# A gated decoder trunk on one core: the gating input projection by Strassen's seven products, its weight sums made by transfers in two parts

## The chip, the core and the metric

The kernel runs on one core of a Trainium2 chip. The metric is the device time of one execution in microseconds (us), as the median of several runs. The engines are TensorE (PE, with its weight loads as PEld), VectorE (DVE), ScalarE (ACT), GpSimd (POOL) and SyncE (SP, which here only starts transfers). "Bank" is one of the eight 128 x 512 accumulation banks of the tile `ps`.

## The reference, cut to what matters

The trunk has two layers on 512 tokens of 1024 channels: a conformer convolution with its feed-forward, then a chunked gating unit with its feed-forward, each followed by a residual sum and a layer normalization. The part that the change touches:

```python
def chunked_spatial_gating(x, w_in, b_in, ln_g, ln_b, w_s, b_s, w_out, b_out):
    z = jax.nn.gelu(x @ w_in + b_in, approximate=False)
    u, v = jnp.split(z, 2, axis=-1)
    v = layer_norm(v, ln_g, ln_b)
    ...
    s = jnp.einsum("gts,bnsgc->bntgc", w_causal, v) + b_s.T[:, :, None]
    s = s.reshape(bsz, t, GMLP_HALF)
    return (u * s) @ w_out + b_out
```

`x @ w_in` is 512 x 1024 by 1024 x 2048. Its second half of columns gives `v` (here "the first projection", since the kernel computes it first), its first half gives `u`.

## The kernel before, in words

All products keep float32 accuracy by splitting: ACT writes a rounded high part (`his`), DVE subtracts it for the low part (`los`), and PE does three matmuls (high-high, high-low, low-high) for each 128 x 128 by 512 block.

**Weights** are a stream of units of 128 x 1024. SP loads unit u into slot u mod 4 of `raw` once the low part of unit u-4 is written; `his` and `los` put its parts into `wh` and `wl`, rings of four, or, around a normalization, into early places (`eh`, `el`). PE signals `w_used` after each unit, which frees the ring slot. All queues are written out by hand, one block for each engine, and run in order.

**Strassen before the change.** The down projections of both feed-forwards are already done with seven products in place of eight. They need sums of weight quarters, made in device memory (`summed`) by transfers: plain copies from SP (`copies`), then accumulating transfers from POOL (`summed_weights`), paced by `w_used` during the up projection.

**The gating stage.** After the second normalization (n = 1) PE transposes the four token tiles of `res` back to feature-major (`block_fm`, 8 transposes each); ACT writes their high parts (`block_hi`), DVE their low parts (`block_lo`). Then PE does the first projection: `down_by_block(U_GV, 4, 4, ...)` for 512 columns, one token tile after another, 24 matmuls each, with the last two `block_fm` in between; then `down_by_k(U_GV + 4, 4, 0, ...)` for the other 512 columns. That is 8 units and 192 matmuls. DVE adds the bias row into `vtm` (eight additions of 128 x 512), ACT applies Gelu, DVE takes the statistics, and normalizes `v` tile by tile into `vh`, `vl`. Meanwhile PE does the second projection (`up`, eight units of 24 matmuls, `U_GU`), whose last two are each followed by two groups of the spatial product (`spatial`), and the first of these waits for all of `vl`. In the middle of the first projection DVE also adds the output bias row to `res` (`residual(2)`).

The quarters are named A11, A12, A21, A22 for tokens by input channels (second index: channels), and the same indices for the weights.

## Time and profile before

| | us |
|---|---|
| median of 3 runs (lowest, highest) | 1015.83 (1014.35, 1017.22) |
| profiled execution, its own time | 1015.58 |
| its span (first to last instruction) | 1013.8 |
| PE busy | 1003.6 |
| DVE busy | 867.6 |
| ACT busy | 604.5 |
| POOL busy | 233.3 |

Busy times are sums over the whole span. A matmul of 128 x 512 is shown as 389 ns long, but the next one starts 227 ns after it, so the duration of a row is not its price on PE; the distance of two starts is. A measurement tells a difference of about 0.3% from none.

### The profile page before, as it was taken

To read this page: it belongs to the slowest core of one execution; us is meant where nothing else is said; L and a number is where in the kernel's file an instruction comes from. 1 tells how busy PE (TensorE), PEld (TensorE's weight loads), DVE (VectorE), ACT (ScalarE), POOL (GpSimd) and SP (SyncE) were. 2 spreads that over 40 slices of the span, in tenths; PEclk is the share of its full clock that TensorE was granted. 3 is DMA by queue.
4 is the path that set the end of the run, shared out by engine and by line. 5 is a ranking of instruction groups with operands and counts; after the bars stand their busy time and mean duration, and the time that the engine had idled before them with its cause. 6 is when DMAs were issued, how large, how long until landed. Compare 5 with 4: busy or idle time off the path is not lost.

```text
span 1013.8 us, 15746 instructions
## 1 busy us (share of the span) xinstructions
PE 1003.6 (99%) x5379; PEld 861.1 (85%) x5379; DVE 867.6 (86%) x1228; ACT 604.5 (60%) x903; POOL 233.3 (23%) x289
## 2 busy tenths in 40 slices
PE   9999999999999999999999999999999999999997
PEld 7777788988899988888888888898988999888885
DVE  6999977897988988898894878779888888879888
ACT  7889865564565556666454343457555555566653
POOL 2998730023232121000010210002423212100001
PEclk9999999999999999999999999999999999999999
DMA  9766269369889676376555333825989966627652
GB/s 342 218 161 166 58 147 349 119 196 238 236 211 228 220 169 173 102 271 208 195 179 194 118 111 107 307 79 186 262 237 229 220 209 173 163 98 260 205 197 112
DMA packets 65590, 194.02 MB, mean 191 GB/s; under 512 B 7552, under 2 KB 8576, under 8 KB 65024
## 3 DMA queue, kind: packets, MB, share of 16 engines
q1 hardware_dynamic: 44144, 137.76, 39.1%
q0 software_dynamic: 19376, 48.24, 23.7%
q10 hardware_dynamic: 2016, 7.34, 2.1%
q8 instruction: 28, 0.46, 0.2%
q14 instruction: 26, 0.21, 0.1%
HBM read 178.11 MB, written 54.53 MB: 229 GB/s over the span
## 4 chain that ended last, share of the span: by engine, by line
PE 78%; DVE 5%; DMA 3%; issue 2%; ACT 1%; SPq 0%; DVEq 0%; POOL 0%; POOLq 0%; ACTq 0%
PE ps L2017 10%; PE ps L2018 10%; PE ps L2019 10%; PE ps L2306 6%; PE ps L2307 6%; PE ps L2308 6%; PE ps L2259 5%; PE ps L2260 5%; PE ps L2261 5%; PE ps L2027 4%; PE ps L2028 4%; PE ps L2029 4%; DMA raw<-d_weights 3%; PE ps L2186 1%; DVE ps L1618 1%
## 5 line engine op out<-in xcount | busy, mean ns | idle before, releaser
L2017 PE MATMUL ps<-xh,wh 128*128 128x512 f32 x528 | 208.5, 395 | 0.3 <-DVE wl L1280 0.3
L2018 PE MATMUL ps<-xl,wh 128*128 128x512 f32 x528 | 205.7, 390 | 0.0
L2019 PE MATMUL ps<-xh,wl 128*128 128x512 f32 x528 | 205.6, 389 | 0.0
L767 ACT ACTIVATE wh<-raw 128x1024 fp32r<-128x1024 f32 x114 | 119.9, 1057 | 80.4 <-PE ps L2308 49.5
L1280 DVE TENSOR_TENSOR wl<-raw,wh 128x1024 fp32r<-128x1024 f32 x101 | 123.2, 1224 | 32.9 <-ACT wh L767 32.5
L702 POOL DMA_DIRECT2D summed<-d_weights x88 | 75.2, 1115 | 198.0 <-PE ps L2019 96.4
L2017 PEld LDWEIGHTS ps<-xh,wh 128*128 128x128 f32 x528 | 99.2, 188 | 22.0 <-issue 1.2
L2019 PEld LDWEIGHTS ps<-xh,wl 128*128 128x128 f32 x528 | 99.1, 188 | 21.0
L2018 PEld LDWEIGHTS ps<-xl,wh 128*128 128x128 f32 x528 | 99.2, 188 | 20.7 <-issue 1.2
L2306 PE MATMUL ps<-wh,parts 128*128 128x512 f32 x264 | 102.9, 390 | 0.0
L2308 PE MATMUL ps<-wh,parts 128*128 128x512 f32 x264 | 102.7, 389 | 0.0
L2307 PE MATMUL ps<-wl,parts 128*128 128x512 f32 x264 | 102.7, 389 | 0.0
L1607 DVE TENSOR_TENSOR wl<-raw,wh 128x1024 fp32r<-128x1024 f32 x62 | 75.6, 1220 | 22.5 <-ACT wh L1014 22.5
L599 POOL TENSOR_SCALAR veps<-sqs 128x1 f32<-128x1 f32 x15 | 4.8, 323 | 385.2 <-ACT squares_down L961 266.2
L1376 DVE SCALAR_TENSOR_TENSOR ps<-glu,par,ps 128x512 f32<-128x512 f32 x125 | 84.7, 752 | 0.6 <-PE ps L2103 0.4
L622 POOL TENSOR_TENSOR gsum<-gsum,prods 128x512 f32<-128x512 f32 x53 | 70.2, 1324 | 14.5 <-ACT prods L836 8.4
L1014 ACT ACTIVATE wh<-raw 128x1024 fp32r<-128x1024 f32 x62 | 65.6, 1058 | 8.2 <-DMA raw<-d_weights 8.2
L1618 DVE SCALAR_TENSOR_TENSOR ps<-vpad,par,ps 128x512 f32<-128x512 f32 x80 | 60.3, 753 | 8.0 <-ACT ps L1038 2.2
L1618 DVE SCALAR_TENSOR_TENSOR ps<-gpad,par,ps 128x512 f32<-128x512 f32 x80 | 60.2, 753 | 6.4 <-DVE ps L1618 2.1
L2306 PEld LDWEIGHTS ps<-wh,parts 128*128 128x128 f32 x264 | 49.5, 188 | 11.1 <-DVE wl L1280 0.8
L2308 PEld LDWEIGHTS ps<-wh,parts 128*128 128x128 f32 x264 | 49.5, 188 | 10.4
L2307 PEld LDWEIGHTS ps<-wl,parts 128*128 128x128 f32 x264 | 49.6, 188 | 10.2
(266 smaller groups left out, 2543.9 us busy)
## 6 DMA issues: line engine op xcount, KB each, us to landing
raw<-d_weights SPq DMA_DIRECT2D x156, 512.0 KB, 4.9
raw<-summed SPq DMA_DIRECT2D x56, 512.0 KB, 4.1
summed<-d_weights POOLq DMA_DIRECT2D x88, 256.0 KB, 9.5
summed<-d_weights SPq DMA_DIRECT2D x66, 256.0 KB, 5.2
...
```

The source lines that it names most:

```text
L702: eng.dma_start(out, of, accum_op=ALU.add).then_inc(w_sum[i % AHEAD], 16)
L767: eng.activation(split_at(u)[0], raw[:, u % RAW, :], ACT.Copy).then_inc(w_hi, 1)
L1280: eng.tensor_tensor(l, raw[:, u % RAW, :], h.bitcast(f32), ALU.subtract).then_inc(w_lo, 1)
L1376: eng.scalar_tensor_tensor(out=ps[:, bank, :], in0=glu[:, j % 2, k:k + SEQ], scalar=par[:, c:c + 1], in1=ps[:, bank, :], op0=ALU.mult, op1 ...
L1607: eng.tensor_tensor(wl[:, slot, :], raw[:, part, :], wh[:, slot, :].bitcast(f32), ALU.subtract).then_inc(w_lo, 1)
L1618: eng.scalar_tensor_tensor(out=accs[v], in0=buf[:, off:off + SEQ], scalar=par[:, bass.ds(cw, 1)], in1=accs[v], op0=ALU.mult, op1=ALU.add). ...
L2017: eng.matmul(ps[:, bank, cols], a, xh[:, k, cols], start=(k == 0), stop=False)
L2018: eng.matmul(ps[:, bank, cols], a, xl[:, k, cols], start=False, stop=False)
L2019: mm = eng.matmul(ps[:, bank, cols], b, xh[:, k, cols], start=False, stop=(k == KD - 1))
L2306: eng.matmul(ps[:, bank + t, :], s_h, w_h[:, cols], start=first, stop=False)
L2307: eng.matmul(ps[:, bank + t, :], s_h, w_l[:, cols], start=False, stop=False)
L2308: mm = eng.matmul(ps[:, bank + t, :], s_l, w_h[:, cols], start=False, stop=last)
```

## The change

The first projection is done with Strassen's seven products (in Winograd's form): quarters of 256 tokens by 512 channels and of 512 channels by 512 columns, seven products of 24 matmuls each. The products need four sums of token quarters (`gn5` = A21 - A22, `gs2` = `gn5` - A11, `gs4` = `gs2` + A12, `gv7` = `gs2` + A22) and sums of weight quarters. The stream has 14 units for the projection in place of 8. The weight sums are made by transfers: SP copies three quarters during the convolution (`gv_copies`), POOL adds into them after the first normalization, and goes on behind the feed-forward's own sums. The first unit of the second projection moves in between the products, to bridge the making of the token sums. The bias addition to `res` moves from DVE to four accumulating transfers of POOL.

```diff
+GQ = KD // 2
+U_GU0 = U_GV + GQ + 2
+U_G56 = U_GU0 + 1
+U_G37 = U_G56 + GQ
+U_GU = U_G37 + GQ - 1
...
+        def gv_copies(i):
+
+            w1, w2 = weights_d[raw_gv + i], weights_d[raw_gv + GQ + i]
+            eng.dma_start(gsum_d[2 + i, :, 0:HALF], w1[:, 0:HALF]).then_inc(gv_copied, 16)
+            eng.dma_start(gsum_d[2 + GQ + i, :, HALF:UNIT], w2[:, 0:HALF]).then_inc(gv_copied, 16)
+            eng.dma_start(gsum_d[2 + GQ + i, :, 0:HALF], w2[:, HALF:UNIT]).then_inc(gv_copied, 16)
...
+            if 0 <= u - U_CONV_OUT < GQ:
+                gv_copies(u - U_CONV_OUT)
```

POOL, around the feed-forward's own sums, and in the gating stage:

```diff
+        eng.wait_ge(gv_copied, 16 * 3 * GQ)
+        eng.dma_start(fifth[:, :, first], w2[:, :, first], accum_op=ALU.add).then_inc(gv_sum, 16)
+        eng.dma_start(third[:, :, second], w2[:, :, second], accum_op=ALU.add).then_inc(gv_sum, 16)
+        eng.wait_ge(gv_sum, 16 * 2)
+        eng.dma_start(fifth[:, :, second], fifth[:, :, first]).then_inc(gv_sum, 16)
         up_sums(0)
+        eng.wait_ge(gv_sum, 16 * 3)
+        eng.dma_start(fifth[:, :, second], w2[:, :, second], accum_op=ALU.add).then_inc(gv_sum, 16)
...
+        for t in range(NT):
+            eng.dma_start(res[:, t, :], brow[:, :], accum_op=ALU.add).then_inc(res3_add, 16)
+        eng.wait_ge(w_used, U_GV + GQ)
+        eng.wait_ge(x_kept, 2 * NT)
+        eng.wait_ge(*lo_of(U_G56 + 1))
+        for t in range(NT // 2):
+            cols = slice(t * P, (t + 1) * P)
+            eng.wait_ge(ga_sum, 2 * t + 2)
+            eng.wait_ge(a22_kept, t + 1)
+            eng.tensor_tensor(gs4[:, :, cols], gs2[:, :, cols], a12f[:, :, cols], ALU.add).then_inc(ga_more, 1)
+            eng.tensor_tensor(gv7[:, :, cols], gs2[:, :, cols], a22f[:, :, cols], ALU.add).then_inc(ga_more, 1)
```

ACT, after the last `block_hi`:

```diff
+        eng.activation(brow[:, :], brow[:, :], ACT.Copy, scale=1.0 / ALPHA).then_inc(br3_ok, 1)
+        token_hi(gn5h, gn5, 0, ga_sum, 1)
+        token_hi(gs2h, gs2, 0, ga_sum, 2)
+        his([U_G56])
+        token_hi(gn5h, gn5, 1, ga_sum, 3)
+        token_hi(gs2h, gs2, 1, ga_sum, 4)
+        his([U_G56 + 1])
+        gelu_v(0, 0, G_C11 - 1)
+        gelu_v(1, 0, G_C11)
+        row(glb[:, :], R_GLB, gm_in)
+        his([U_G56 + 2])
+        gelu_u(0)
+        his([U_G56 + 3])
```

DVE, after the token sums:

```diff
+        token_lo(gn5l, gn5, gn5h, 0, 1)
+        token_lo(gs2l, gs2, gs2h, 0, 2)
+        los([U_G56])
+        los([U_G56 + 1])
+        token_lo(gn5l, gn5, gn5h, 1, 3)
+        token_lo(gs2l, gs2, gs2h, 1, 4)
+        los([U_G56 + 2])
+        eng.wait_ge(w_used, U_GU0)
+        eng.wait_ge(rows_ok, 1)
+        for t in halves:
+            eng.tensor_tensor(vtm[:, 2 + t, c2], vtm[:, 2 + t, c1], both_rows[:, :], ALU.subtract).then_inc(n_ok, 1)
+        eng.wait_ge(n_ok, NT // 2)
+        for t in halves:
+            eng.tensor_tensor(vtm[:, 2 + t, c1], ps[:, 4 + t, :], vtm[:, 2 + t, c1], ALU.add).then_inc(gv_rd, 1)
+        los([U_G56 + 3])
```

PE, after the products A11 x B11 and A12 x B21 (24 matmuls and a `block_fm` for each of two token tiles) and the product with A22 (24 matmuls):

```diff
+        up(split_at(U_GU0), GU_BANK[0]).then_inc(w_used, 1)
+        for pair in range(GQ // 2):
+            for t in range(NT // 2):
+                eng.wait_ge(ga_lo, 2 * t + 2)
+                for i in (2 * pair, 2 * pair + 1):
+                    u = U_G56 + i
+                    if t == 0:
+                        eng.wait_ge(*lo_of(u))
+                    gv(u, 0, 0, gn5p, i, t)
+                    mm = gv(u, 1, 2, gs2p, i, t)
+                    if t == 1:
+                        mm.then_inc(w_used, 1)
...
+        for i in range(GQ):
+            gv_third(i)
+            if i < GQ - 2:
+                gv_seventh(i)
```

Three places show what the change does to the order on the engines. On DVE in the gating stage, from the last normalized tile on, it stood like this before (`vtm` holds the projection, `wl<-raw,wh` is a `los`):

```order
L1772 SCALAR_TENSOR_TENSOR res<-scaled_down,rstd,brow_n 128x1024 [waits rstd_ok,nrm]
L1532 TENSOR_TENSOR xl<-ps,xh 128x4x128 [waits x_hi] x4
L1943 TENSOR_TENSOR vtm<-ps,gvrow 128x512 [waits blk,gv_in]
L1280 TENSOR_TENSOR wl<-raw,wh 128x1024 [waits w_hi,w_used]
L1943 TENSOR_TENSOR vtm<-ps,gvrow 128x512 [waits blk]
L1280 TENSOR_TENSOR wl<-raw,wh 128x1024 [waits w_hi,w_used]
L1948 BN_STATS stats<-vtm 128x6 [waits v_gelu]
```

After the change the same place reads as follows, from the second token tile's part of the sums on (`gn_133` is `gn5`, `gs_134` is `gs2`):

```order
L2091 TENSOR_TENSOR gs_134<-gn_133,a11f 128x4x128 [waits ga_sum]
L2070 TENSOR_TENSOR gn5l<-gn_133,gn5h 128x4x128 [waits ga_hi,ga_sum]
L2070 TENSOR_TENSOR gs2l<-gs_134,gs2h 128x4x128 [waits ga_hi]
L1407 TENSOR_TENSOR wl<-raw,wh 128x1024 [waits w_hi,w_used] x2
L2070 TENSOR_TENSOR gn5l<-gn_133,gn5h 128x4x128 [waits ga_hi]
L2070 TENSOR_TENSOR gs2l<-gs_134,gs2h 128x4x128 [waits ga_hi]
L1407 TENSOR_TENSOR wl<-raw,wh 128x1024 [waits w_hi,w_used]
L2103 TENSOR_TENSOR vtm<-vtm,both_rows 128x512 [waits rows_ok,w_used]
L2103 TENSOR_TENSOR vtm<-vtm,both_rows 128x512
L2106 TENSOR_TENSOR vtm<-ps,vtm 128x512 [waits n_ok]
L2106 TENSOR_TENSOR vtm<-ps,vtm 128x512
L1407 TENSOR_TENSOR wl<-raw,wh 128x1024 [waits w_hi,w_used]
```

The low part of the fourth of these units (the last row, `U_G56 + 3`) now stands behind six operations on the tokens and on `vtm`. On POOL, between the roots of the second normalization and the mask of the spatial weights, there was nothing; now there stand four transfers and four additions (`gs_135` is `gs4`, `gv_136` is `gv7`):

```order
L639 TENSOR_TENSOR rstd<-veps,half_m 128x1 [waits eps_ok]
L814 DMA res<-brow 128x1024 [waits xt,x_ok,br3_ok]
L814 DMA res<-brow 128x1024 x3
L822 TENSOR_TENSOR gs_135<-gs_134,a12f 128x4x128 [waits ga_sum,w_lo,a22_kept,x_kept,w_used]
L823 TENSOR_TENSOR gv_136<-gs_134,a22f 128x4x128
L822 TENSOR_TENSOR gs_135<-gs_134,a12f 128x4x128 [waits a22_kept,ga_sum]
L823 TENSOR_TENSOR gv_136<-gs_134,a22f 128x4x128
L826 AFFINE_SELECT wsraw<-wsraw 128x1024 [waits gm_in]
```

What moved here is work that DVE did before (the addition of the row) or that is new; DVE's queue holds the rest. On ACT, from the last high parts of the tokens on, it now reads:

```order
L1063 ACTIVATE a22f<-ps 128x4x128 [waits x_lo]
L855 DMA bsrow<-d_rows 128x1024 [waits x_ok]
L855 DMA grow<-d_rows 128x1024
L855 DMA brow_n<-d_rows 128x1024
L1343 ACTIVATE brow<-brow 128x1024 [waits bo_in]
L1327 ACTIVATE gn5h<-gn_133 128x4x128 [waits ga_sum]
L1327 ACTIVATE gs2h<-gs_134 128x4x128 [waits ga_sum]
L850 ACTIVATE wh<-raw 128x1024 [waits raw_in2,w_used]
L1327 ACTIVATE gn5h<-gn_133 128x4x128 [waits ga_sum]
L1327 ACTIVATE gs2h<-gs_134 128x4x128 [waits ga_sum]
L850 ACTIVATE wh<-raw 128x1024 [waits raw_in3,w_used]
L1332 ACT_TABLE_LOAD
```

Before, this stretch of ACT held six row transfers and the table load, then Gelu and `his` in turn; the high parts of the token sums and three more weight units now go through it.

## Rows read from the trace of the kernel before

**Rows 1.** The page: the span, and PE's busy time.

```profile
span 1013.8 us, 15746 instructions
PE 1003.6 (99%) x5379; PEld 861.1 (85%) x5379; DVE 867.6 (86%) x1228; ACT 604.5 (60%) x903; POOL 233.3 (23%) x289
```

**Rows 2.** PE's waits between 480 and 640 us: total, times, longest.

```profile
PE ps L2351 <- DVE wl L1280: 0.2, 1, 0.2
```

**Rows 3.** Timeline of PE in the gating stage: start, us, engine, line, what.

```profile
537.90 0.47 PE L2027 MATMUL ps<-eh,xh 128*128 128x512 f32 x1
...
538.68 0.39 PE L2027 MATMUL ps<-eh,xh 128*128 128x512 f32 x1
...
560.44 0.39 PE L2027 MATMUL ps<-wh,xh 128*128 128x512 f32 x1
```

**Rows 4.** Timeline of DVE in the gating stage, with idle time before.

```profile
533.79 1.29 DVE L1772 SCALAR_TENSOR_TENSOR res<-scaled_down,rstd,brow_n 128x1024 f32<-128x1024 f32 x1 [0.89 <-POOL rstd L588]
...
538.38 1.29 DVE L1532 TENSOR_TENSOR xl<-ps,xh 128x512 fp32r<-128x512 f32 x2 [2.11 <-ACT xh L967]
...
565.64 2.35 DVE L1280 TENSOR_TENSOR wl<-raw,wh 128x1024 fp32r<-128x1024 f32 x2
```

**Rows 5.** Timeline of ACT in the gating stage (ACTq: transfers it starts).

```profile
539.52 0.45 ACTq L772 DMA_DIRECT2D bsrow<-d_rows  x1
...
541.40 1.28 ACT L1232 ACT_TABLE_LOAD   x1 [2.56 <-issue]
...
555.58 2.00 ACT L767 ACTIVATE wh<-raw 128x1024 fp32r<-128x1024 f32 x2
...
571.57 1.23 ACT L1232 ACTIVATE vtm<-vtm 128x512 f32<-128x512 f32 x2 [5.10 <-DVE vtm L1943]
```

**Rows 6.** DVE and POOL side by side: durations in ns, min/median/max, first and last start.

```profile
L743 POOL TENSOR_SCALAR_AFFINE_SELECT wsraw<-wsraw x1: 1680/1680/1680, 559.6 to 559.6; 128x1024 f32<-128x1024 f32 x1
L1548 DVE SCALAR_TENSOR_TENSOR res<-res,brow x4: 1214/1214/2124, 560.2 to 564.5; 128x1024 f32<-128x1024 f32 x4
L588 POOL TENSOR_TENSOR rstd<-veps,half_m x2: 538/540/543, 528.4 to 533.1; 128x1 f32<-128x1 f32 x2
L588 POOL TENSOR_TENSOR rstd<-veps,half_m x4: 1407/1462/1558, 578.2 to 584.6; 128x1 f32<-128x1 f32 x4
```

**Rows 7.** POOL's additions of 128x512 in the convolution, columns as above.

```profile
L622 POOL TENSOR_TENSOR gsum<-gsum,prods x53: 1270/1296/2317, 21.0 to 111.8; 128x512 f32<-128x512 f32 x53
```

**Rows 8.** Timeline of DVE: v's normalization from first to last, and the first use of the spatial product.

```profile
577.90 1.27 DVE L1962 SCALAR_TENSOR_TENSOR vtm<-vtm,mv,glg 128x1024 f32<-128x1024 f32 x1
...
597.86 1.23 DVE L1970 TENSOR_TENSOR vl<-vtm,vh 128x1024 fp32r<-128x1024 f32 x1
...
609.79 0.69 DVE L1982 TENSOR_TENSOR vtm<-ps,bsrow 128x512 f32<-128x512 f32 x1 [3.34 <-PE ps L2401]
```

**Rows 9.** Convolution: timelines of POOL, SP and PE.

```profile
90.06 0.87 POOL L613 DMA_DIRECT2D wl<-raw  x1
96.91 0.80 SPq L532 DMA_DIRECT2D raw<-d_weights  x2
99.04 0.48 PE L2017 MATMUL ps<-xh,wh 128*128 128x512 f32 x1
```

**Rows 10.** Stretch: length, busy of PE, PEld, DVE, ACT, POOL; clock, DMA share, GB/s.

```profile
150.00:180.00 30.00, 29.70 (x143) 24.36 (x142) 24.28 (x38) 17.94 (x29) 2.23 (x6) 1.00 0.99 335
```

**Rows 11.** Timeline of POOL: its first weight sums, and its return after the last.

```profile
217.86 5.95 POOL L702 DMA_DIRECT2D summed<-d_weights  x7 [32.77 <-issue]
510.45 0.19 POOL L599 TENSOR_SCALAR veps<-sqs 128x1 f32<-128x1 f32 x1 [120.22 <-ACT squares_down L961]
```

**Rows 12.** Stretches at the end of the program, columns as in Rows 10.

```profile
1006.00:1008.00 2.00, 1.00 (x5) 0.49 (x3) 1.97 (x4) 0.08 (x1) 0.00 (x0) 1.00 0.65 260
1008.00:1010.00 2.00, 0.00 (x0) 0.00 (x0) 1.72 (x5) 0.73 (x2) 0.88 (x2) 0.87 0.66 268
```

**Rows 13.** Weight loads from start to landing at 516 to 625 us.

```profile
DMA to landing us min/median/max: 3.0/3.3/6.0
```

310 lines of the change are left out of this document (235 added, 75 removed).

## The prediction, made before the changed kernel ran

> **What bounds the kernel now.** I read the page first: PE is busy for 1003.6 of a span of 1013.8 us [rows 1], DVE for 867.6. Then PE's waits in the stretch of the change, 480 to 640 us: one, of 0.2 us [rows 2]. So here the time is PE's instruction stream and nothing else, and DVE and ACT only have to be early enough. The price of a matmul is the distance of starts: 96 of them between 538.68 and 560.44 us, 0.2267 us each [rows 3]. All sums are made in the profiled execution (span 1013.8, its own time 1015.58) and carried to the median 1015.83, which is 0.25 us above it. About 0.3%, 3.05 us, is what a measurement tells from no change.
>
> **What PE saves.** The first projection falls from 192 to 168 matmuls; transposes, second projection and spatial products stay. 24 x 0.2267 = 5.44 us. This is the most that the change can give, and it is given only if PE never waits for the new work.
>
> **What is added.** Six more weight units: six loads, six `his` on ACT (two in 2.00 us [rows 5], 1.0 each) and six `los` on DVE (two in 2.35 us [rows 4], 1.15 apart). On DVE: twenty reads of banks and rows into `vtm` in place of eight, four token differences, eight low parts of token sums, all of 128x512 (two in 1.29 us [rows 4], 0.6 apart), less the four `residual` additions of 1.2 us: 6 x 1.15 + 24 x 0.6 - 4.9 = 16.4 us more. On ACT: 6 x 1.0 and about 15 short ones at 0.6. Both engines have room in total; what counts is the order.
>
> **PE's needs after the change.** Up to 537.90 us, where the last transposes end [rows 3], PE's stream is the same length. Then, with 24 matmuls as 5.44 us: the product with A22 from 537.9 to 543.4, the moved unit to 548.9, the first half of products five and six to 554.4, six matmuls of the second half to 555.8, and there it needs the low part of unit `U_G56 + 3`.
>
> **DVE and ACT up to there.** The last `normed` starts at 533.79 because it waits 0.89 us for its root [rows 4]; the first `vtm` addition fits into that gap. Then one addition (0.6), `block_lo` of tile 2 (1.2) and two `los` bring DVE to 539.1 and the last `block_lo` to 540.3. The unit for A22 is there at 538.0 and the last tile 0.5 us before PE asks for it: I take 0.2 us of wait here. Two additions and a `los` end at 542.7, four token differences at 545.4.
> ACT copies A22's second tile until 541.1, starts three row transfers (539.52 to 541.40 before, 1.9 us [rows 5]) until 543.0, scales `brow` until 544.0, and then does two token parts and a unit (546.2), two and a unit (548.4), the table load of 1.28 us, two Gelus of together 1.23, a transfer's start (0.4, nearest row 0.45) [rows 5] and the third unit: 552.4. DVE follows: the second unit's low part at 549.6, when PE wants it at 550.3. So far no wait.
> Without anything in its way DVE would then do two token parts (550.8), the third unit (552.5 to 553.6), two subtractions with `both_rows` (554.8), two bank additions (556.1) and the fourth unit: 557.3. PE would wait 1.5 us, from 555.8.
>
> **But POOL is in its way.** POOL's additions `gs4` and `gv7` wait for that same second low part, so all four start at 549.6 (the four transfers ahead, 0.9 us each by the nearest POOL issue [rows 9], are done by 548). The nearest row of such an addition is 1.296 us [rows 7]. What happens beside DVE: the mask on POOL ran from 559.55 to 561.23, and the DVE addition with both inputs in SBUF that started at 560.2 took 2.124 us against 1.214 for the other three, ending about as late as if it had begun when POOL was done. The other way too: POOL's roots take 0.54 us, and 1.41 to 1.56 while DVE runs such instructions [rows 6]. So the two take turns. The Trainium skill, SBUF — State Buffer, section "Who interferes with whom", has the rule: a DVE instruction with two SBUF inputs and a GpSimd instruction that reads SBUF exclude each other, and the second to issue blocks fully. The trace agrees, with its 0.91 us.
> Token parts, `los` and the `both_rows` subtractions all have two SBUF inputs. In turns, 1.15 us for each POOL addition and 0.55 or 1.1 for each DVE one: first token part 550.1, POOL 551.3, second token part 551.9 (PE wanted it at 551.7: 0.2 us), POOL 553.0, third unit 554.1 (in time for 554.6), POOL 555.3, subtraction 555.9, POOL 557.0, subtraction 557.6, bank additions (no SBUF pair, free) 558.8, fourth unit 560.1. PE comes to it at 556.0 and waits 4.1 us.
>
> **After it.** PE goes on at 560.1, does 18 matmuls to 564.2. POOL's last sum at 557.0 gives ACT's part at 558 and two units by 560.1; DVE has four token parts and two `los` done at 564.8, the first of these at 563.7, in time. The seventh product ends at 575.1; DVE reads its banks until 577.5, and two more units, a pair of statistics ahead, are in time by over 1.5 us. Loads land in 3.3 us, at most 6.0 [rows 13]; with the 2 MB of residual transfers beside them they may take longer, and the first that could hurt is needed 6 us after it is issued. From 577.5 DVE has a unit, six statistics, a unit and the aggregates (1.15 + 3.6 + 1.15 + 0.4) before v's normalization, which starts at 583.8; its 21.2 us, 577.90 to 599.1 before [rows 8], then end at 605.0. PE starts the spatial product after six units, 575.1 + 32.6 = 607.7, which leaves 2.7 us. (Before, DVE saw it at 609.79 [rows 8].)
>
> **The transfers.** The twelve copies start with units 16 to 19 in the convolution. The low part of units 14 and 15 is itself a transfer of POOL, issued at 90.06, and is down at 96.91, when SP goes on; PE uses it from 99.04 [rows 9]: 2.1 us to spare. Six copies, 1.57 MB, fall just ahead of it; at 335 GB/s, the rate of the busiest stretch with such copies [rows 10], they take 4.7 us, of which some 3.4 fit into idle transfer time: 1.3 us late, still in time. I cost it at nothing, with 2 us at the worst. The second piece has POOL's 32.77 idle us up to 217.86 for about 3 MB, the third its 120 idle us up to 510.45 [rows 11]. Both are hidden; POOL would have to be 15 us slower to be late with the feed-forward's own sums.
>
> **The sum.** -5.44 + 0.2 + 0.2 + 4.1 = -0.9 us: 1014.9 us. Both ends for the unknown price of the turns: nothing (the wait is 1.5), or all four additions in full with DVE idle meanwhile (5.2 more, the wait 6.7). Net -3.7 to +1.5.
>
> **The rivals.**
> *DVE is not held up* (chance 0.30): the additions on POOL start later than I think, or are short beside DVE, as the median of 1.296 us with a busy DVE in the convolution could hint; there DVE's instructions read a bank, though. Then -5.44 + 0.2 + 1.5 = -3.7: 1012.1 us, and 1011 if ACT is half a microsecond earlier at each row transfer.
> *The clock falls during the wait* (0.18), which decides for slower. At the end of the program PE stops at 1007.0 and the mean clock between 1008 and 1010 is 0.87 [rows 12], so it fell to its half, 1.2 GHz, at 1009.5, after 2.5 us without a matmul. A wait of 4.1 us in the middle may do the same, and each matmul at the lower level costs 0.227 us more. Twelve of them give 1017.6, a whole unit of 24 gives 1020.3; from 18 on (4.0 us over -0.9) the kernel is slower than before by more than 3.05 us. Against it: the wait is short, and PE was at its full rate up to it.
> *The copies in the convolution hold up unit 14* (0.10): 2 us or more on top, 1017 us.
>
> **The numbers.** Forecast as reckoned 0.42, own range 1013.3 to 1016.5. Faster by over 0.3%: most of the first rival and the lower edge of the forecast, 0.32. Slower: half of the clock's case, half of the copies', a little of the forecast, 0.16. Within 0.3%: 0.52. Range 1011.3 to 1018.0.
>
> **What would show it.** 24 fewer matmuls, surely. PE: one idle time of 3 to 5 us before a matmul that waits for the low part of unit `U_G56 + 3`, some 18 us after the last transposes; under 1.5 us there and the first rival holds. POOL's four additions and DVE's token parts and `los` between 549 and 558 us: durations stretched to about twice show the turns, plain 0.7 and 1.2 refute them. Clock under 1.00 behind the wait: the second rival. PE idle at about 99 us for `wl<-raw`: the third. I am wrong altogether if PE waits longest elsewhere: at the A22 product, or at the spatial product for v.

## The result, and the profile after

| | before | after |
|---|---|---|
| median of six executions each, us | 1015.49 | 1020.77 |
| lowest, highest | 1014.35, 1017.22 | 1017.82, 1023.90 |
| profiled execution, its own time | 1015.58 | 1017.82 |
| its span | 1013.8 | 1016.0 |

The ratio is 1.0052, with a 95% interval of 1.0032 to 1.0072. The change costs about 5.3 us (3.2 to 7.3), where I forecast a gain of 0.9. The profiled execution of the kernel after is the fastest of its six, 3 us under their median, and the one before lies at its median; what is read from the two traces is therefore compared piece by piece below, and not by their total times. The page of the kernel after, beside [rows 1]:

```profile
span 1016.0 us, 15812 instructions
PE 999.7 (98%) x5355; PEld 858.0 (84%) x5355; DVE 887.9 (87%) x1254; ACT 618.9 (61%) x924; POOL 256.6 (25%) x310
```

PE has its 24 matmuls less and is busy for 3.9 us less, and the span is longer all the same. So time went into waits, or lies where PE no longer works. PE's waits between 500 and 640 us (total, times, longest), beside [rows 2]:

```profile
PE ps L2579 <- DVE wl L1407: 3.1, 1, 3.1
PE ps L2537 <- DVE wl L1407: 1.0, 2, 0.7
PE ps L2579 <- DVE el L1407: 0.9, 1, 0.9
```

The first is the wait that the prediction named: low part of unit `U_G56 + 3`. PE's timeline around it:

```profile
555.79 0.39 PE L2581 MATMUL ps<-wh,gs2l 128*128 128x512 f32 x1
559.32 0.65 PE L2579 MATMUL ps<-wh,gn5h 128*128 128x512 f32 x1 [3.15 <-DVE wl L1407]
559.77 0.63 PE L2580 MATMUL ps<-wl,gn5h 128*128 128x512 f32 x1
...
562.75 0.48 PE L2581 MATMUL ps<-wh,gn5l 128*128 128x512 f32 x1
563.07 0.39 PE L2579 MATMUL ps<-wh,gs2h 128*128 128x512 f32 x1
```

Two things are to be seen. The next matmul starts 3.53 us after the last one, 3.30 more than the usual 0.23. And then the starts stand 0.43 us apart, not 0.23, up to 563.07: nine steps took 3.75 us where nine times 0.2267 are 2.04, so 1.71 us are lost behind the wait. The stretches of the same place (length, busy of PE, PEld, DVE, ACT, POOL; clock, DMA share, GB/s) show the reason in the clock:

```profile
555.00:560.00 5.00, 1.85 (x8) 1.21 (x7) 4.97 (x7) 2.84 (x5) 1.26 (x1) 0.95 1.06 277
560.00:565.00 5.00, 5.00 (x17) 3.94 (x17) 4.04 (x5) 1.06 (x1) 0.00 (x0) 0.71 1.04 282
```

A distance of 0.43 us is that of the lower of the clock's two levels, 1.2 GHz, and 0.23 that of the higher, 2.4 GHz.

What made PE wait is on DVE, whose timeline stands beside POOL's here:

```profile
548.79 0.68 DVE L2070 TENSOR_TENSOR gn5l<-gn,gn5h 128x512 fp32r<-128x512 f32 x1
549.39 1.78 DVE L2070 TENSOR_TENSOR gs2l<-gs,gs2h 128x512 fp32r<-128x512 f32 x1
551.10 2.31 DVE L1407 TENSOR_TENSOR wl<-raw,wh 128x1024 fp32r<-128x1024 f32 x1
553.33 3.48 DVE L2103 TENSOR_TENSOR vtm<-vtm,both_rows 128x512 f32<-128x512 f32 x2
556.85 1.29 DVE L2106 TENSOR_TENSOR vtm<-ps,vtm 128x512 f32<-128x512 f32 x2
558.05 1.22 DVE L1407 TENSOR_TENSOR wl<-raw,wh 128x1024 fp32r<-128x1024 f32 x1
...
549.10 1.52 POOL L822 TENSOR_TENSOR gs<-gs,a12f 128x512 f32<-128x512 f32 x1 [2.48 <-issue]
550.59 1.73 POOL L823 TENSOR_TENSOR gv<-gs,a22f 128x512 f32<-128x512 f32 x1
552.28 2.27 POOL L822 TENSOR_TENSOR gs<-gs,a12f 128x512 f32<-128x512 f32 x1
554.52 1.74 POOL L823 TENSOR_TENSOR gv<-gs,a22f 128x512 f32<-128x512 f32 x1
```

The merged row of the two subtractions, taken apart (durations in ns, min/median/max):

```profile
L2103 DVE TENSOR_TENSOR vtm<-vtm,both_rows x2: 1780/1780/1781, 553.3 to 555.0; 128x512 f32<-128x512 f32 x2
```

While POOL's four additions run, DVE's instructions take 1.78 in place of 0.68, 2.31 in place of 1.22, and each of the two subtractions 1.78 in place of 0.68: 1.1 us for each of the four additions. And each ends 0.55 us (128 x 512) or 1.1 us (128 x 1024) after the addition beside it has ended, about what it takes alone. That is taking turns, as forecast. The bank additions start at 556.85, when POOL's last addition has ended (556.26), so their plain length says nothing about turns. The rule of the Trainium skill on which the forecast leaned (SBUF — State Buffer, section "Who interferes with whom") holds here for POOL's tensor_tensor against DVE instructions with two SBUF inputs.

The loss that was not forecast at all begins 50 us earlier, with the second normalization. The same rows of DVE's timeline, of the kernel before, and then of the kernel after with POOL's row beside them:

```profile
505.45 0.69 DVE L1782 SCALAR_TENSOR_TENSOR res<-ps,res 128x512 f32<-128x512 f32 x1 [0.33 <-PE ps L2308]
...
509.11 0.42 DVE L1800 TENSOR_TENSOR parts<-made,parts 128x256 fp32r<-128x256 f32 x1
509.45 0.68 DVE L1782 SCALAR_TENSOR_TENSOR res<-ps,res 128x512 f32<-128x512 f32 x1
```

```profile
503.61 0.69 DVE L1909 SCALAR_TENSOR_TENSOR res<-ps,res 128x512 f32<-128x512 f32 x1 [0.33 <-PE ps L2494]
...
507.28 1.52 DVE L1927 TENSOR_TENSOR parts<-made,parts 128x256 fp32r<-128x256 f32 x1
508.72 0.68 DVE L1909 SCALAR_TENSOR_TENSOR res<-ps,res 128x512 f32<-128x512 f32 x1
...
506.45 2.07 POOL L807 TENSOR_TENSOR both_rows<-gvrow 128x512 f32<-128x512 f32 x1 [91.81 <-PE ps L2494]
```

The kernel after comes to this place 1.84 us early and leaves it 0.73 early. In between, an operation of 0.42 us took 1.52, beside POOL's sum of the two halves of the bias row: turns again. The rest follows on PE (before, then after):

```profile
518.60 0.60 PE L2186 MATMUL ps<-ident,res 128*128 128x128 f32 x4
...
530.70 0.55 PE L2186 MATMUL ps<-ident,res 128*128 128x128 f32 x3
```

```profile
517.88 1.03 PE L2372 MATMUL ps<-ident,res 128*128 128x128 f32 x8
...
527.58 0.50 PE L2579 MATMUL ps<-eh,xh 128*128 128x512 f32 x1 [0.93 <-DVE el L1407]
...
531.11 1.03 PE L2372 MATMUL ps<-ident,res 128*128 128x128 f32 x8
...
538.24 0.48 PE L2579 MATMUL ps<-wh,xh 128*128 128x512 f32 x1
...
1006.57 0.39 PE L2539 MATMUL ps<-xh,parts 128*128 128x512 f32 x1
```

0.72 us early at the first transposes, 0.41 late at the third; between them is a wait of 0.93 us for `el`, the low part of `U_GV + 3`. The last matmul starts at 1006.57, and before at 1006.61: inside the program the whole gain of 5.44 us has been given back. And behind it there is one loss more. The rows of the program's last line, before and after (engine, duration in ns three times, start):

```profile
L2426 POOLq DRAIN  x1: 3749/3749/3749, 1009.3 to 1009.3; - x1
...
L2426 SPq DRAIN  x1: 7/7/7, 1013.6 to 1013.6; - x1
L2426 SPq EVENT_SEMAPHORE  x1: 17/17/17, 1013.8 to 1013.8; - x1
```

```profile
L2680 POOLq DRAIN  x1: 6650/6650/6650, 1009.2 to 1009.2; - x1
...
L2680 SPq DRAIN  x1: 7/7/7, 1013.5 to 1013.5; - x1
L2680 SPq EVENT_SEMAPHORE  x1: 17/17/17, 1016.0 to 1016.0; - x1
```

POOL's last instruction starts at the same time and takes 6.65 us in place of 3.75. In the kernel before it ended at 1013.03, ahead of SP's last instruction at 1013.6; now all engines wait for it at the program's end, and the span ends 9.5 us after the last matmul's start in place of 7.2 (2.24 us more).

The ledger of the two profiled executions, from 505 us on: +1.11 (bias row on POOL), +1.14 (`el`), -0.07 up to 538.24, -5.44 (24 matmuls), +3.30 (wait), +1.71 (clock), +2.24 (POOL's last instruction) is +3.99. The kernel after had come to 505 us 1.84 us early, which leaves 2.15; the spans differ by 2.2. That head start is chance: the second trace of the same kernel (a1 below) was 3.6 us late from 268 us on. But behind 500 us it says the same as the first: from there to the last matmul it loses 1.82 us against the kernel before, the first trace 1.80, and each loses 2.24 or 2.25 more at the end.

### The profile page after: what moved, and what is told of

Read it like the earlier page. It is cut to its first block, busy times and chain, and to the rows that moved or that the text cites. A ratio compares the mean times of both kernels' runs of the same rounds, so it can differ in the third digit from the quotient of the medians.

```text
span 1016.0 us, 15812 instructions
## 1 busy us (share of the span) xinstructions
PE 999.7 (98%) x5355; PEld 858.0 (84%) x5355; DVE 887.9 (87%) x1254; ACT 618.9 (61%) x924; POOL 256.6 (25%) x310
## 4 chain that ended last, share of the span: by engine, by line
PE 80%; DVE 6%; issue 2%; DMA 1%; ACT 1%; POOL 0%; DVEq 0%; POOLq 0%; ACTq 0%
PE ps L2204 11%; PE ps L2205 11%; PE ps L2206 11%; PE ps L2446 6%; PE ps L2447 6%; PE ps L2445 6%; PE ps L2492 6%; PE ps L2493 6%; PE ps L2494 6%; PE ps L2214 2%; PE ps L2215 2%; PE ps L2216 2%; DVE wl L1407 1%; PE ps L2579 1%; PE ps L2372 1%
## 5 line engine op out<-in xcount | busy, mean ns | idle before, releaser
L850 ACT ACTIVATE wh<-raw 128x1024 fp32r<-128x1024 f32 x120 | 126.0, 1057 | 82.5 <-PE ps L2494 49.5
L1407 DVE TENSOR_TENSOR wl<-raw,wh 128x1024 fp32r<-128x1024 f32 x107 | 131.0, 1231 | 21.9 <-ACT wh L850 21.9
L1729 DVE TENSOR_TENSOR wl<-raw,wh 128x1024 fp32r<-128x1024 f32 x62 | 75.6, 1220 | 19.8 <-ACT wh L1104 19.8
L1104 ACT ACTIVATE wh<-raw 128x1024 fp32r<-128x1024 f32 x62 | 65.5, 1057 | 7.0 <-DMA raw<-d_weights 7.0
```

Source lines behind the costliest of these rows:

```text
L850: eng.activation(split_at(u)[0], raw[:, u % RAW, :], ACT.Copy).then_inc(w_hi, 1)
L1407: eng.tensor_tensor(l, raw[:, u % RAW, :], h.bitcast(f32), ALU.subtract).then_inc(w_lo, 1)
L1729: eng.tensor_tensor(wl[:, slot, :], raw[:, part, :], wh[:, slot, :].bitcast(f32), ALU.subtract).then_inc(w_lo, 1)
```

## The experiments

The kernel before ran beside each of them, and ratios are to its runs there; its medians lay between 1015.21 and 1015.94 us (1014.41 beside f3, a single execution). The theory: DVE and POOL take turns, that gives the long wait, the clock's fall hangs on the wait, and something of its own lengthens the program's end. The rival: the transfers of the sums cost the time, by contention in the convolution, at the loads, and at the end.

**a1_again.** The changed kernel once more, unchanged.

> The changed kernel once more, with nothing altered, for a second trace of it. By every theory about 1020.8 us, 5 us over before. Turn theory (DVE and POOL exclude each other, PE waits for the low part of unit U_G56 + 3, then its clock falls): the same wait of 3 us before that unit's first matmul and a clock below 1.00 behind it, together some 5 us. Load theory (the four residual transfers hold up weight loads): the high parts of the three units after it come 2 to 5 us late, and how late differs from execution to execution, which would explain that most executions took 3 us more than the profiled one.

Measured: 1021.25 us, ratio 1.0050 (1.0036 to 1.0064). The wait was 3.16 us, and seven matmuls behind it stood 0.43 us apart. The loss is real, and the wait is the same in both traces.

**a2_lo_first.** The low part of `U_G56 + 3` ahead of the bias subtractions and bank additions on DVE:

```diff
         los([U_G56 + 2])
+        los([U_G56 + 3])
...
-        los([U_G56 + 3])
```

> One line of DVE's queue moved: the low part of unit U_G56 + 3 stands right behind that of U_G56 + 2, ahead of the two subtractions with both_rows and the two bank additions. Turn theory: the low part is written about 3 us earlier, the wait shrinks from 3.1 us to under 1 us, and the clock stays at 1.00; 4 to 5 us faster than the changed kernel, about 1016. Load theory: its high part waits for its load until 553.5 us anyway, so PE gains only 1.5 to 2 us at that unit and then meets the next late units: 1018 to 1020.

Measured: 1020.88 us, ratio 1.0037 (1.0023 to 1.0051). The one wait became four of 0.77, 1.79, 0.79 and 0.67 us, 4.0 in all, and no matmul was slow. The order on DVE alone moves the wait; what DVE has to do up to the third product is too long. The clock is gained, but its gain went into the new waits: from 500 us to the last matmul this trace loses 1.99 us, no less than the changed kernel's 1.80.

**a3_late_res.** The residual's four transfers behind the roots of v's normalization:

```diff
-        for t in range(NT):
-            eng.dma_start(res[:, t, :], brow[:, :], accum_op=ALU.add).then_inc(res3_add, 16)
         eng.wait_ge(w_used, U_GV + GQ)
...
             mixer_root(ROOTS + 2 * NT + t, ROOTS + t + 1, t, 1)
+        for t in range(NT):
+            eng.dma_start(res[:, t, :], brow[:, :], accum_op=ALU.add).then_inc(res3_add, 16)
```

> The four residual transfers of POOL stand behind the roots of v's normalization, some 45 us later; nothing else. Turn theory: DVE's queue is as long as before and the wait before unit U_G56 + 3 stays near 3 us, the time stays within 1.5 us of the changed kernel's 1020.8. Load theory: loads land in 3 to 5 us again in place of 10 to 13, no high part waits for a load between 550 and 565 us, and the typical time falls by the 3 us by which most executions exceeded the profiled one, to about 1017.5.

Measured: 1021.76 us, ratio 1.0058 (1.0044 to 1.0071), with the wait still 3.14 us. The loads of weights between 538 and 560 us, from start to landing (least, median, most), first in the changed kernel and then in this one:

```profile
DMA to landing us min/median/max: 3.2/10.6/13.1
```

```profile
DMA to landing us min/median/max: 3.3/5.1/8.9
```

The transfers slow the loads to twice their time, but these are not what PE waits for. This one also shows that the wait alone doesn't decide the clock:

```profile
560.61 0.50 PE L2579 MATMUL ps<-wh,gn5h 128*128 128x512 f32 x1 [3.14 <-DVE wl L1407]
560.94 0.40 PE L2580 MATMUL ps<-wl,gn5h 128*128 128x512 f32 x1
```

With the same waits as the changed kernel and without the fall, this trace loses 0.19 us from 500 us to the last matmul, where the changed kernel loses 1.80. That puts the price of the fall at 1.6 us. In the other executions of this kernel it seems to have fallen: their mean granted clock is 0.994 in three and 0.996 in one, against 0.997 in the profiled one, and they took 3 to 6 us longer. No trace of them shows where.

**a4_fill.** Thirty small matmuls of no use, so that PE isn't idle in the wait:

```diff
                     if t == 0:
+                        if i == GQ - 1:
+                            busy(30, 7)
                         eng.wait_ge(*lo_of(u))
```

> PE does 30 transposes of the identity into a free bank (some 3 us of otherwise idle time) just before it waits for the low part of unit U_G56 + 3; they change no result. If the fall of the clock costs what the trace shows (nine matmuls at 0.43 in place of 0.23 us), this kernel is 1.7 to 2 us faster than the changed one although PE does more work, with the clock at 1.00 throughout; if the clock is no cause, it is equal or slower by up to 0.5 us.

Measured: 1019.97 us, ratio 1.0030 (1.0018 to 1.0041). The wait left was 0.6 us, and the clock stood at 1.00 in every stretch from 540 to 570 us. About 1.3 us against a1 come back in the medians, though the intervals overlap. In the trace the nine steps behind the wait are 1.5 us shorter, but 1.2 us of it went again at 576 and 578 us, where PE waited for low parts whose loads had come late (ACT waited 2.7 and 0.7 us for them). So the fall costs what it costs only where the next units are ready.

This execution was also the slowest of its ten, 1023.88 us, for a reason that has nothing to do with the edit. In the convolution, just where the prediction's third rival expected it, PE waited for the low part of unit 14, and the clock fell behind that wait too. The row of the wait, and the stretch behind it (columns as above):

```profile
102.55 0.50 PE L2204 MATMUL ps<-xh,wh 128*128 128x512 f32 x1 [2.12 <-DMA wl<-raw]
...
103.00:107.00 4.00, 4.00 (x12) 3.08 (x11) 4.00 (x7) 3.44 (x9) 1.92 (x2) 0.57 0.89 207
```

**b1_sums_only.** The rival alone: the kernel before with the sums' transfers and nothing that uses them.

```diff
             load(u % RAW, u)
+            if 0 <= u - U_CONV_OUT < GQ:
+                gv_copies(u - U_CONV_OUT)
...
+        eng.dma_start(fifth[:, :, first], w2[:, :, first], accum_op=ALU.add).then_inc(gv_sum, 16)
+        eng.dma_start(third[:, :, second], w2[:, :, second], accum_op=ALU.add).then_inc(gv_sum, 16)
...
         up_sums(0)
...
+        eng.dma_start(fifth[:, :, second], w2[:, :, second], accum_op=ALU.add).then_inc(gv_sum, 16)
...
```

> The kernel before, with the transfers of the weight sums added and nothing that uses them: SP's twelve copies in the convolution, GpSimd's three transfers at the first normalization and its ten behind the feed-forward's own sums. No computation differs from before. If the transfers cost nothing, as the prediction had it: 1015.5, ratio 1.000, and the program's last instruction comes about 7.2 us after the last matmul's start. If GpSimd's last instruction lengthens with the number of transfers that it issued (it took 3.75 us before, 6.65 us in each version of the changed kernel), this kernel ends some 2 us later, 1017.5, with matmuls that end as before. If the copies in the convolution hold up units 14 and 15 as well, some 1 to 2 us more at 105 us in some executions, 1018 to 1019.

Measured: 1018.33 us, ratio 1.0021 (1.0011 to 1.0031), 2.1 us. POOL's last instruction took 6.49 us, and the program ended 9.39 us behind the last matmul's start: 2.2 us more than before, which is the whole of the measured difference. (POOL's queue carries 167 transfers here, twelve more than before, where the expectations count thirteen.) In this trace the transfers cost nothing ahead of the last matmul, so the end part of the rival stands. Its contention part is not settled by this one trace. Between 90 and 115 us, where SP's copies run, the matmuls keep to the time of the kernel before within 0.02 us in all five other traces without the copies. In the fourteen traces with them they lose 0.7 us on average: nothing or 0.1 in six of them, 0.4 to 1.0 in six, 1.8 in a7 and 4.0 in a4, and every wait there is for `wl<-raw`. So the copies do cost something, in some executions and not in others.

**a5_no_sums.** The other way round: the changed kernel without them.

```diff
-                gv_copies(u - U_CONV_OUT)
...
-            return gsum_d[u - U_GV - GQ]
+            return weights_d[raw_gv + u - U_GV]
...
-            return gsum_d[u - U_G56 + 2]
+            return weights_d[raw_gv + (u - U_G56) % KD]
```

> The changed kernel without the transfers of the weight sums: units that read a sum load a plain block of the weights instead, so the gating's first projection multiplies by wrong weights, with the same number of loads, splits and matmuls. If the transfers carry part of the loss (GpSimd's last instruction 2.25 us, copies in the convolution about 1 us): 1017.5 to 1018.5. If they carry none, 1020.8. The wait for the low part of the fourth unit of the sums, 3.1 us, and the slower clock behind it stay in both cases.

Measured: 1019.11 us, ratio 1.0038 (1.0025 to 1.0052). All PE waits of the stage were as in the changed kernel (3.1, 0.9, 0.7), and POOL's last instruction took 6.49 us still. That was against my expectation for the end: without any transfer for the sums, the four residual transfers that remain are enough. The 2 us against a1 are within what the intervals leave open. As in a3 the clock stood at 1.00 behind a wait of 3.14 us, and from 500 us to the last matmul this trace loses 0.15 us.

**a6_rows_late.** POOL's sum of the bias row's halves behind the residual's transfers:

```diff
-        eng.wait_ge(gv_in, 16)
-        eng.wait_ge(w_used, U_GV - FOURTH)
-        eng.tensor_tensor(both_rows[:, :], gvrow[:, 0:HALF], gvrow[:, HALF:D], ALU.add).then_inc(rows_ok, 1)
         for t in range(NT):
             norm_root(ROOTS + NT + t, NT + t + 1, t)
...
+        eng.wait_ge(gv_in, 16)
+        eng.tensor_tensor(both_rows[:, :], gvrow[:, 0:HALF], gvrow[:, HALF:D], ALU.add).then_inc(rows_ok, 1)
```

> The changed kernel with GpSimd's sum of the two halves of the bias row moved from the start of the second normalization (506 us) to behind the residual's transfers (about 546 us). If that one instruction, 2.07 us beside VectorE's 128x256 operation that grew from 0.42 to 1.52 us, puts VectorE's whole normalization 1.1 us late: TensorE's shift between 500 and 531 us, +1.1 and +1.2 us, falls to under 0.5 in all and the time to 1018.8 to 1019.8, unless the sum now falls beside VectorE's work on the token sums and gives 1 us back there. If the shift comes from elsewhere (the bias row's load, the weights' loads): it stays, 1020.8.

Measured: 1021.56 us, ratio 1.0057 (1.0041 to 1.0073). The operation `parts<-made,parts` was back at 0.42 us, and TensorE's shift of 1.1 us between 505 and 518 us was gone; the wait for `el`, 0.9 us, stayed, so it has another cause. At its new place POOL's sum (second row) took turns again, and one DVE operation of 0.69 us (first row) took 2.57:

```profile
545.81 2.57 DVE L2090 TENSOR_TENSOR gs<-gn,a11f 128x512 f32<-128x512 f32 x1
...
546.55 2.96 POOL L813 TENSOR_TENSOR both_rows<-gvrow 128x512 f32<-128x512 f32 x1
```

PE's waits for `wl` rose to 5.0 us, 3.7 the longest. From 500 us to the last matmul this trace loses 3.49 us, 1.7 more than the changed kernel, although the 1.1 are gone: a cost that is moved into DVE's crowded stretch is paid there more than in full.

**a7_token_sums_dve.** The four token sums by DVE, and no longer by POOL:

```diff
+        for t in halves:
+            cols = slice(t * P, (t + 1) * P)
...
+            eng.tensor_tensor(gs4[:, :, cols], gs2[:, :, cols], a12f[:, :, cols], ALU.add).then_inc(ga_more, 1)
+            eng.tensor_tensor(gv7[:, :, cols], gs2[:, :, cols], a22f[:, :, cols], ALU.add).then_inc(ga_more, 1)
         eng.wait_ge(w_used, U_GU0)
```

> The changed kernel with the four token sums gs4 and gv7 formed by VectorE, ahead of its wait for the fourth product, instead of by GpSimd (1.5 to 2.3 us each there, between 549 and 556 us). If the two engines take turns in these operations, VectorE's own stretched ones (1.78 and 2.31 us, 0.69 and 1.22 alone, 3.48 for two subtractions) shrink by some 4 us while the four added ones cost about 2.8 us, and the wait of TensorE for the low part of the fourth unit falls from 3.1 to about 2: 1019 to 1020. If there are no turns and the long operations have another reason, VectorE's work is 2.8 us longer and so is the wait: about 6 us, 1024.

Measured: 1019.99 us, ratio 1.0043 (1.0028 to 1.0059). DVE's timeline, in place of the stretched one above:

```profile
552.93 0.68 DVE L2061 TENSOR_TENSOR gs2l<-gs,gs2h 128x512 fp32r<-128x512 f32 x1
...
554.60 1.23 DVE L1398 TENSOR_TENSOR wl<-raw,wh 128x1024 fp32r<-128x1024 f32 x1 [0.98 <-ACT wh L841]
555.75 0.68 DVE L2095 TENSOR_TENSOR gs<-gs,a12f 128x512 f32<-128x512 f32 x1
```

No operation is stretched: the turns are shown from both sides. The wait fell to 2.22 us, with no slow matmul behind it. Four additions of 0.60 us on DVE are cheaper than four of 1.5 to 2.3 in turns, but not by much, and now ACT waited 2.17 us, until 557.25, for the load of `U_G56 + 3`, so that the load was next.

**c1_one_transfer, c2_semaphores, f3_one_row, g1_one_fewer.** What lengthens POOL's last instruction? The kernel before with one transfer more on POOL's queue (c1: 256 KB, f3: one row), with twelve unused semaphores (c2), and with a transfer less (g1). The edit of c1:

```diff
         up_sums(0)
+        eng.dma_start(more_d[:, 0:HALF], weights_d[0, :, 0:HALF]).then_inc(more, 16)
```

> The kernel before with one more transfer on GpSimd's queue (a plain copy of 256 KB that nobody reads, behind the first feed-forward's sums): 156 transfers in place of 155. GpSimd's last instruction took 3.75 us in the kernel before (155 transfers on its queue), 6.49 in the changed kernel without the sums' transfers (159) and in the kernel before with them (168), 6.65 in the changed kernel (171). If it goes by the number of GpSimd's transfers, in steps: a step between 155 and 159 may lie here, 6.5, or just not, 3.75. If it goes by their bytes or packets: 3.75 to 4.0.

> The kernel before with twelve more semaphores that nothing uses. If GpSimd's last instruction goes by the number of semaphores of the program (two more in the kernel before with the sums' transfers, some fourteen in the changed kernel), it takes about 6.5 us here; if it goes by transfers, 3.75.

> The kernel before with one more transfer on GpSimd's queue, of one row of 2 KB: 156 transfers, but hardly more bytes or packets than before (19376 packets on that queue). If GpSimd's last instruction goes by the number of transfers, 6.5 us as in c1_one_transfer; if by packets or bytes (19456 packets in c1), 3.75.

> The kernel before with 154 transfers on GpSimd's queue: the residual of the last token tile ahead of the first normalization doesn't get its bias row, which is left out of the computation. If GpSimd's last instruction is short up to 155 transfers of this program: 3.75 us. If the kernel before with its 155 is a single case: 5.9 to 7.1 us.

One execution each. POOL's last instruction, in c1, f3, c2 and g1:

```profile
L2429 POOLq DRAIN  x1: 6483/6483/6483, 1007.8 to 1007.8; - x1
```

```profile
L2429 POOLq DRAIN  x1: 6487/6487/6487, 1008.7 to 1008.7; - x1
```

```profile
L2427 POOLq DRAIN  x1: 3749/3749/3749, 1008.1 to 1008.1; - x1
```

```profile
L2426 POOLq DRAIN  x1: 3749/3749/3749, 1009.4 to 1009.4; - x1
```

A single transfer more, even of one row, is the whole step of 2.7 us; twelve semaphores more do nothing. It isn't bytes.

**d1_mend.** Four edits against four losses: the bias row's sum by a transfer, TensorE taking both products of a unit at once, token sums on DVE, and the third unit of the sums for both token tiles ahead of the fourth.

```diff
-        eng.wait_ge(w_used, U_GV - FOURTH)
-        eng.tensor_tensor(both_rows[:, :], gvrow[:, 0:HALF], gvrow[:, HALF:D], ALU.add).then_inc(rows_ok, 1)
+        eng.dma_start(gvrow[:, HALF:D], gvrow[:, 0:HALF], accum_op=ALU.add).then_inc(rows_ok, 16)
...
                 mm = gv(U_GV + i, 0, 4, g11, i, t)
-            mm.then_inc(gv_pe, 1)
-            eng.wait_ge(c_rd, R_P4 + 1 + t)
-            for i in range(GQ):
+                if i == GQ - 1:
+                    mm.then_inc(gv_pe, 1)
                 mm = gv(U_GV + i, 1, 6, g12, i, t)
...
-        for pair in range(GQ // 2):
+        for units in ((0, 1), (2,), (3,)):
```

> The changed kernel with four edits, each against one loss: the sum of the bias row's halves by an accumulating transfer in place of GpSimd's instruction (1.1 us); TensorE takes each unit of the first product at once with its other half in the second product, so that U_GV+3 is needed as late as before (el wait, 0.9 to 1.2 us); the token sums by VectorE (0.5 us); the third unit of the sums for both token tiles ahead of the fourth (six matmuls more before the wait, 1.4 us, and with a shorter wait perhaps a clock that doesn't fall, 1.7 us). If these readings are right: 1021 - 1.1 - 1.1 - 0.5 - 1.4 - 0 to 1.7 = 1015.2 to 1016.9. If VectorE's work is the bound of the stage however it is ordered, the waits only move and it ends at 1018 to 1020. GpSimd's last instruction still takes 6.5 us or more in either case.

Measured: 1019.87 us, ratio 1.0047 (1.0033 to 1.0061), 3 us above what I expected. The shift of 1.1 us, the wait for `el` and the slow matmuls were gone, but there were four waits for `wl`: 1.64, 1.11, 0.57 and 0.86 us.

**d2_mend_more.** As d1, with the residual's transfers late as in a3, and with these two moves (ACT, then DVE; the second `los` goes in between the two halves of the token sums):

```diff
+        his([U_G56 + 2])
         gelu_v(0, 0, G_C11 - 1)
         gelu_v(1, 0, G_C11)
         row(glb[:, :], R_GLB, gm_in)
-        his([U_G56 + 2])
...
+        los([U_G56 + 3])
+        for t in (1,):
```

> The kernel of d1 with the residual's four transfers behind the roots of the gating's normalization, ScalarE's high part of the third unit ahead of its two Gelu, and VectorE's low part of the fourth unit ahead of half of the token sums and of the bank additions. If what is left of the wait for the fourth unit is its load, which landed at 557.2 beside the residual's transfers with ScalarE waiting 2.17 us for it, the wait falls under 0.5 us: 1 to 2 us better than d1, 1013.5 to 1015.5. If it is VectorE's total work, the same as d1, with waits at the next units instead.

Measured: 1016.53 us, ratio 1.0010 (1.0002 to 1.0019). PE didn't wait at the fourth unit at all; 1.64 us at 540 and 1.12 us at the third product were left. In a3 the late transfers gained nothing, and here the step from d1, of which they are one part of three, gained 3.3 us. Together with the 2.17 us for which ACT waited for a load in a7 this speaks for two causes one behind the other, turns first and loads next; which of the three parts gained how much was not separated.

**h4_fewer and e4_best.** Fewer transfers on POOL's queue, 144 in place of 171 (h4), and the same in d2 with 145 and one more move (e4): plain copies within the sums are replaced by base copies on SP's queue.

```diff
+            half = slice(HALF, UNIT) if i % 2 else slice(0, HALF)
+            eng.dma_start(to[2 * KQ + i // 2, :, half], w1[:, HALF:UNIT]).then_inc(w_copied[i], 16)
...
-                    issue(i, fourth_sum(to, i), to[i, :, second])
...
-                    issue(i, fourth_sum(to, i), w1[i, :, second], ALU.add)
+                    issue(i, fourth_sum(to, i), to[i, :, second], ALU.add)
```

> The changed kernel with 144 transfers on GpSimd's queue in place of 171: plain copies of sums are replaced by base copies of a block of the weights on SyncE's queue, onto which GpSimd's transfer adds the rest (7 transfers for the gating's sums in place of 12, 22 fewer for the feed-forwards' sums). If GpSimd's last instruction goes by the number: 3.75 us, the last instruction of the program 7.2 us behind the last matmul's start, 1020.8 - 2.25 = 1018.5. If only the sums' total matters: 6.5 us still, 1020.8.

> The kernel of d2_mend_more with 145 transfers on GpSimd's queue (in the manner of h4_fewer, one more for the bias row), and on VectorE the low parts that the third product needs ahead of the bias subtractions and bank additions, with TensorE's wait for these behind the first unit of the third product. From d2's 1016.5: last instruction -2.25, wait at the third product (1.12 us) -1.0: 1013.2, ratio 0.998, faster than the kernel before, if the causes found are the whole loss and the last instruction goes by the number of transfers. If it doesn't: 1015.5. If VectorE bounds the stage and the wait only moves on: 1 us more in each case.

Measured: 1030.98 us, ratio 1.0146 (1.0130 to 1.0161), and 1027.31 us, ratio 1.0111 (1.0096 to 1.0125). Both expectations failed, for the end and for the total. POOL's last instruction took 5.92 and 7.14 us, so it doesn't simply go by the number of transfers either. And the base copies, which I had taken for free, cost about 10 us between 243 and 277 us: loads of weights between 225 and 285 us took 3.4/10.6/21.5 us to land (least, median, most) in h4 against 3.8/6.6/12.8 in the kernel before, and PE stood for 5.45 us in one piece. The clock fell in that wait, with a mean of 0.51 between 268 and 275 us in h4, which makes up to 3 of the 10. More copies on the queue that also brings the weights were the worst edit of all.

**e5_best.** As d2, with DVE's low parts for the third product ahead of the bias work, and PE's wait for a free bank one unit later:

```diff
+        for t in halves:
+            token_lo(gs4l, gs4, gs4h, t, 4 + 2 * t + 1)
+            token_lo(gv7l, gv7, gv7h, t, 4 + 2 * t + 2)
+        los([U_G37])
...
-        eng.wait_ge(gv_rd, G_MP4)
         for i in range(GQ):
             gv_third(i)
+            if i == 0:
+                eng.wait_ge(gv_rd, G_MP4)
```

> The kernel of d2_mend_more with VectorE's low parts for the third product, and of its first unit, ahead of the bias subtractions and bank additions, and TensorE's wait for these behind the first unit of the third product. GpSimd's transfers as in d2 (172), so its last instruction stays at 6.7 us. From d2's 1016.5: the wait of 1.12 us at the third product gone, 1015.4, the same as the kernel before. If VectorE bounds the stage and the wait moves on to the next units: 1016.5.

Measured: 1015.99 us, ratio 1.0008 (0.9999 to 1.0017). The wait of 1.12 us was down to 0.28. The longest was now 1.64 us at 542, and it is one of my own edits: with both products of a unit taken together, the first one ends later for the second token tile, DVE's bank addition waits 1.91 us for it, and the low parts queued behind it are late.

**e6_best.** Both products of a unit together for the first token tile alone:

```diff
-                mm = gv(U_GV + i, 1, 6, g12, i, t)
-                if t == 1:
-                    mm.then_inc(w_used, 1)
+                if t == 0:
+                    if i == 0:
+                        eng.wait_ge(c_rd, R_P4 + 1)
+                    gv(U_GV + i, 1, 6, g12, i, t)
+            if t == 1:
+                eng.wait_ge(c_rd, R_P4 + 2)
+                for i in range(GQ):
+                    gv(U_GV + i, 1, 6, g12, i, t).then_inc(w_used, 1)
```

> The kernel of e5_best with TensorE taking the two products of a unit together for the first token tile alone; for the second tile the first product comes whole, as in the changed kernel, so that VectorE's bank addition isn't held back (1.91 us in e5) and U_GV+4's low part, 1.64 us late there, is in time. From e5's 1016.0: -1.6, 1014.4, ratio 0.999 and with it about 1 us faster than the kernel before, although GpSimd's last instruction still takes 6.7 us. If VectorE is the bound of the stage, the wait comes back at the fourth unit or the third product: 1016.

Measured: 1014.06 us, ratio to the kernel before 0.9986 (0.9976 to 0.9995), in the same comparison with 1015.87. PE's waits between 500 and 640 us:

```profile
PE ps L2581 <- DVE wl L1396: 0.2, 1, 0.2
PE ps L2539 <- DVE wl L1396: 0.2, 1, 0.2
```

So the losses found in the stage are nearly all of them: with each undone, the change is 1.8 us faster than before by the medians (1.4 by the ratio), even with POOL's last instruction still at 6.69 us.

The traces say it piece by piece. The table compares the start of the same matmul, counted from the first, with the kernel before: what is lost (+) from 90 to 115 us, from 500 us to the last matmul, and from there to the end of the span.

| run | 90 to 115 us | 500 us to last matmul | behind it |
|---|---|---|---|
| changed kernel | 0.0 | +1.80 | +2.24 |
| a1_again | 0.0 | +1.82 | +2.25 |
| a2_lo_first | +1.0 | +1.99 | +2.24 |
| a3_late_res (clock stayed) | 0.0 | +0.19 | +2.25 |
| a4_fill | +4.0 | +1.57 | +2.24 |
| a5_no_sums (clock stayed) | 0.0 | +0.15 | +2.08 |
| a6_rows_late | +0.1 | +3.49 | +2.24 |
| a7_token_sums_dve | +1.8 | +0.43 | +2.24 |
| b1_sums_only | 0.0 | 0.0 | +2.17 |
| d1_mend | 0.0 | +1.01 | +2.28 |
| d2_mend_more | +0.5 | -1.84 | +2.28 |
| e5_best | +0.5 | -2.30 | +2.29 |
| e6_best | +0.8 | -4.67 | +2.28 |

e6 gets 4.67 of the 5.44 us back, and pays 2.28 at the end.

## Why the prediction was wrong

**The saving, -5.44: right.** 24 matmuls fewer, at 0.227 us.

**The turns and the wait: right in mechanism, a little large in size.** "One idle time of 3 to 5 us before a matmul that waits for the low part of unit `U_G56 + 3`" is what the profile shows, 3.30 us net for the 4.1 of the sum. PE came to the unit at 556.0, as reckoned. All four of POOL's additions cost DVE 1.1 us (I said 1.15), in the order reckoned; only the whole chain ran 0.7 to 0.8 us early, and its last part ended at 559.3 and not at 560.1. ACT had the second unit ready at 547.55 (I said 548.4), so POOL's additions started at 549.10 (I said 549.6), beside a token part already under way. a7 shows the stretching gone with the additions. The two terms of 0.2 us, A22's unit and the second token part, came to nothing. The rival "DVE is not held up" is refuted, and so is what it drew from the median of 1.296 us in the convolution [rows 7].

**"The clock falls during the wait" (0.18): it did, left out of the sum, for 1.7 us.** This was a rival and should have been in the sum's range: eight matmuls at the lower of the two levels, 1.2 GHz, and one between them, 1.71 us, where I had reckoned with twelve or 24. My reason against it, "the wait is short", was worth little. But it isn't certain either: it fell behind 3.15, 3.16, 3.65 and (in h4) 3.14 us of waiting, and not behind 3.14 in a3 and in a5. Behind shorter waits it fell once, 2.12 us in the convolution of a4, and not behind 2.22 in a7 or 1.79 in a2.

**"Up to 537.90 us, where the last transposes end, PE's stream is the same length": this step failed, for 2.2 us.** The stream is as long, but two things ahead of it changed. I had not costed `both_rows` on POOL at all, although the rule of turns, which I used 40 us later, says what it does beside DVE: 1.11 us, shown by a6. And the products of a quarter take one 128-row half of a unit at a time. Nine matmuls, not eighteen, stand ahead of the one that needs `U_GV + 3`: 9 x 0.227 = 2.04 us earlier. In the kernel before DVE had it at 528.25 and PE came to it at 529.24, 1.0 us to spare, so a wait of 1.0 was to be read there; 0.93 was measured. In d1, d2, e5 and e6, where the eighteen are restored, it is gone.

**"Both are hidden" and the copies "at nothing": nearly right inside the program, wrong at its end, for 2.2 us.** In b1 the sums' transfers cost nothing ahead of the last matmul. The rival of the copies holding up unit 14 (0.10) did not decide the two traces of the changed kernel, but it is no empty one: the copies cost 0.7 us on average between 90 and 115 us, and 4.0 at the worst, a wait of 2.12 us and the clock's fall behind it. "At nothing, with 2 us at the worst" was too little on both counts. But I never asked what the program's end does. POOL's last instruction grew by 2.9 us and now ends last: 2.24 us. This is the largest term of the sum that was not there. No row of [rows 12], which I read for the clock alone, would have given its size, but the rows of the program's last line would have shown that POOL's last instruction ended only 0.6 us ahead of SP's.

**"Loads land in 3.3 us, at most 6.0": wrong, and without effect here.** They took 10.6 us in the median beside the residual's transfers. The reserve behind the fourth unit covered that; it showed as soon as the turns were gone, in ACT's wait of 2.17 us for a load in a7.

The terms: -0.9 as forecast, -0.8 for the wait and -0.4 for the two small ones that weren't there, +1.7 clock, +2.2 ahead of 538 us, +2.2 at the end: +4.0. The measured difference is 5.3 with an interval of 3.2 to 7.3, which holds it. Of the remaining 1.3 us the copies in the convolution are worth 0.7 by the average of the traces, which is an estimate; the rest, or whether it is anything, is open.
